# Prompt attention on one core: the selected branch's scores stand between two groups of transposes, and the compressed branch comes last in a unit

## The reference, cut to what matters

```python
def nsa_chunk(q, gate, qpos, kc, vc, cend, ks_blk, vs_blk, kw, vw, wpos, overlap, rel_bias):
    ...
    s_c = jnp.einsum('bcgqd,bngd->bcgqn', q, kc).astype(jnp.float32) * scale
    ...
    p_c = masked_softmax(s_c, (dist_c >= 0)[None, :, None, None, :])
    o_c = jnp.einsum('bcgqn,bngd->bcgqd', p_c.astype(vc.dtype), vc)
    ...
    s_s = jnp.einsum('bcgqd,bcgkd->bcgqk', q, k_sel).astype(jnp.float32) * scale
    ...
    o_s = jnp.einsum('bcgqk,bcgkd->bcgqd', p_s.astype(v_sel.dtype), v_sel)
    ...
    o_w = jnp.einsum('bcgqw,bwgd->bcgqd', p_w.astype(vw.dtype), vw)
    g = jax.nn.sigmoid(gate.astype(jnp.float32))
    o = g[..., 0:1] * o_c + g[..., 1:2] * o_s + g[..., 2:3] * o_w
    return o.astype(q.dtype)
```

## Time and profile before

| | us |
|---|---|
| median of 3 runs | 1875.83 (1871.49 to 1879.88) |
| the profiled execution, its time | 1881.08 |
| the profiled execution, its span on the core | 1879.3 |
| PE busy / PEld busy / DVE busy / ACT busy | 1772.3 / 1685.5 / 816.1 / 525.9 |
| prompt attention, from the first maximum to the last final | 211.5 to 332.6 |

### The profile page before, as it was taken

One profiled execution on the slowest core, in us unless ns is written; L12 is line 12 of the kernel. 1 busy time (PEld: TensorE's weight loads), 2 busy tenths in 40 slices (PEclk: granted clock), 3 DMA queues, 4 the chain that ended last, 5 costly groups with the idle time before them and its releaser, 6 DMA issues. The chain is left out here.

```text
span 1879.3 us, 35977 instructions
## 1 busy us (share of the span) xinstructions
PE 1772.3 (94%) x15724; PEld 1685.5 (90%) x15724; DVE 816.1 (43%) x1650; ACT 525.9 (28%) x896; POOL 702.7 (37%) x282
## 2 busy tenths in 40 slices
PE   6989788789978998999999999999999999999997
PEld 6987677559856997899999999999999999999997
DVE  4162487223483444465530355443246455024421
ACT  5132365223331222322221222322223222112211
POOL 1200000013213111465553465656565565445541
PEclk8987699889979998899999999999999999999999
DMA  5640330423201000222223222332222222232222
GB/s 146 111 70 23 128 100 24 124 76 92 74 9 47 4 4 27 68 68 90 84 68 96 90 69 64 95 104 75 90 86 72 88 70 74 85 100 81 74 71 77
DMA packets 158252, 140.84 MB, mean 75 GB/s; under 512 B 16170, under 2 KB 153806, under 8 KB 157710
## 3 DMA queue, kind: packets, MB, share of 16 engines
q1 hardware_dynamic: 158094, 138.53, 25.2%
HBM read 132.62 MB, written 10.02 MB: 76 GB/s over the span
## 5 line engine op out<-in xcount | busy, mean ns | idle before, releaser
L271 POOL TENSOR_TENSOR w_lo<-w_raw,w_hi 128x2048 fp32r<-128x2048 f32 (+3 forms) x109 | 458.8, 4209 | 798.8 <-ACT w_hi L265 798.6
L310 PE MATMUL ps<-h_hi,w_hi 128*128 128x288 f32 x1792 | 385.1, 296 | 0.0
L310 PE MATMUL ps<-h_lo,w_hi 128*128 128x288 f32 x1792 | 384.6, 295 | 0.0
L310 PE MATMUL ps<-h_hi,w_lo 128*128 128x288 f32 x1792 | 384.4, 295 | 0.0
L265 ACT ACTIVATE w_hi<-w_raw 128x2048 fp32r<-128x2048 f32 (+3 forms) x109 | 190.0, 1743 | 510.1 <-PE ps L310 460.0
L310 PEld LDWEIGHTS ps<-h_hi,w_hi 128*128 128x128 f32 x1792 | 287.2, 188 | 0.3
L310 PEld LDWEIGHTS ps<-h_lo,w_hi 128*128 128x128 f32 x1792 | 287.2, 188 | 0.0
L310 PEld LDWEIGHTS ps<-h_hi,w_lo 128*128 128x128 f32 x1792 | 287.0, 188 | 0.0
L419 DVE TENSOR_TENSOR xT<-ps,xT 128x576 f32<-128x576 f32 x48 | 35.7, 757 | 265.9 <-PE ps L310 265.9
L310 PE MATMUL ps<-g_hi,w_hi 128*128 128x288 f32 x704 | 151.1, 295 | 0.0
L310 PE MATMUL ps<-g_lo,w_hi 128*128 128x288 f32 x704 | 151.0, 295 | 0.0
(11 more groups left out here) (500 smaller groups left out, 3016.3 us busy)
## 6 DMA issues: line engine op xcount, KB each, us to landing
w_raw<-in_ffn_up SPq DMA_DIRECT2D x44, 1024.0 KB, 5.1
w_raw<-in_ffn_down SPq DMA_DIRECT2D x16, 768.0 KB, 4.8
w_raw<-in_w_in_odd SPq DMA_DIRECT2D x12, 1024.0 KB, 5.1
w_raw<-in_ffn_down SPq DMA_DIRECT2D x16, 640.0 KB, 4.4
w_raw<-in_w_in_even SPq DMA_DIRECT2D x7, 1024.0 KB, 5.4
w_raw<-in_w_in_even SPq DMA_DIRECT2D x6, 872.0 KB, 9.9
BT<-rv SPq DMA_DIRECT2D x8, 520.0 KB, 3.5
seg<-in_cache_cmp_kv SPq DMA_DIRECT2D x32, 128.0 KB
```

What stands on the lines that cost most here:

```text
L271: pool.tensor_tensor(slab_view(wlo[slot], st), slab_view(raw[slot], st), slab_view(whi[slot], st).bitcast(F32), ALU.subtract).then_inc(w_l ...
L310: last = pe.matmul(ps[:, bank + 2 * j + half, 0:HT], w[slot][:, c:c + 128], x[:, xs + t, half * HT:(half + 1) * HT], start=(t == 0 and n = ...
```

## The change

PE's queue in unit u gets another order. The selected transposes come first and signal a semaphore of their own, `pts_ready`. Then come the selected scores of unit u + 2, then the window's transposes and the compressed one (`pt_ready`), then the other scores of u + 2. The outputs are in the order selected, window, compressed, and each waits for its own copy only. ACT copies `PTs` first, on `pts_ready`, and `PTc` second, on `pt_ready`. The selected scores wait for the maximum of unit u instead of u + 1 (their bank alternates with s). DVE's queue keeps its order; its copy `PTw` still waits for `pt_ready`. No matmul, copy or transfer is added or removed.

```diff
-                    def scores(u):
+                    def scores(u, branches):
                         h, qt, s = u // 4, u % 4, u % 2
                         g, hh = h // 4, h % 4
-                        if u >= 1:
-                            pe.wait_ge(s_taken, u)
+                        if u >= 2:
+                            pe.wait_ge(s_taken, u - 1)
...
                         for n, (out, keys) in enumerate(jobs):
+                            if (n == 0) != (branches == "selected"):
+                                continue
+                            if n == 2 and u >= 1:
+                                pe.wait_ge(s_taken, u)
                             if n == 2 and u >= 2:
                                 pe.wait_ge(ptc_act, u - 1)
...
+                        for kt in range(qt + 1):
+                            last = pe.transpose(ps[:, 5, 128 * kt:128 * kt + 128], sS[s][:, 128 * kt:128 * kt + 128], ident[:, :])
+                        last.then_inc(pts_ready, 1)
+                        if u + 2 < U:
+                            scores(u + 2, "selected")
+                        if u >= 1:
                             pe.wait_ge(pt_dve, u)
                         for kt in range(qt + 1):
-                            pe.transpose(ps[:, 5, 128 * kt:128 * kt + 128], sS[s][:, 128 * kt:128 * kt + 128], ident[:, :])
                             pe.transpose(ps[:, 6, 128 * kt:128 * kt + 128], sW[s][:, 128 * kt:128 * kt + 128], ident[:, :])
                         if u + 2 <= U:
                             pe.wait_ge(s_taken, u + 2)
+                        if u >= 1:
+                            pe.wait_ge(ptc_act, u)
                         pe.transpose(ps[0:32, 4, 256:384], sC[s][:, :], ident[:, :]).then_inc(pt_ready, 1)
                         if u + 2 < U:
-                            scores(u + 2)
+                            scores(u + 2, "others")
                         pe.wait_ge(pt_act, u + 1)
-                        pe.wait_ge(pt_dve, u + 1)
                         if u >= 1:
                             pe.wait_ge(o_taken, u)
                         O = ps[:, 7, 0:192]
-                        pe.matmul(O[:, 0:64], PTc[:, :], vc[0:32, 2, 64 * g:64 * g + 64], start=True, stop=True)
                         for n, (PT, c0) in enumerate(((PTs, 896), (PTw, 1152))):
+                            if n == 1:
+                                pe.wait_ge(pt_dve, u + 1)
                             for kt in range(qt + 1):
...
-                        last.then_inc(o_ready, 1)
+                        pe.wait_ge(ptc_act, u + 1)
+                        pe.matmul(O[:, 0:64], PTc[:, :], vc[0:32, 2, 64 * g:64 * g + 64], start=True, stop=True).then_inc(o_ready, 1)
...
-                        act.wait_ge(pt_ready, u + 1)
+                        act.wait_ge(pts_ready, u + 1)
                         if u >= 1:
                             act.wait_ge(o_ready, u)
+                        act.copy(PTs[:, 0:qt + 1, :], ps[:, 5, 0:128 * (qt + 1)].rearrange("p (a b) -> p a b", b=128)).then_inc(pt_act, 1)
+                        act.wait_ge(pt_ready, u + 1)
                         act.copy(PTc[:, :], ps[0:32, 4, 256:384]).then_inc(ptc_act, 1)
-                        act.copy(PTs[:, 0:qt + 1, :], ps[:, 5, 0:128 * (qt + 1)].rearrange("p (a b) -> p a b", b=128)).then_inc(pt_act, 1)
```

More of the change, by code:

```diff
@@ L1531, in load_group @@
                     sp.dma_start(K[1][s2][:, :, :], a["cache_win_kv"][b, 0].rearrange("(t p) k g d -> p t (k g d)", p=128)).then_inc(kvw_in[grp][s2], 16)
-            on_t, on_ev, ptc_act = sem("on_t"), sem("on_ev"), sem("ptc_act")
+            on_t, on_ev, ptc_act, pts_ready = sem("on_t"), sem("on_ev"), sem("ptc_act"), sem("pts_ready")
             U = 4 * NH
@@ L1574, in scores @@
                             last = pe.matmul(out, q, keys[1], start=False, stop=True)
-                        last.then_inc(s_ready, 1)
-                    scores(0)
-                    scores(1)
+                        if branches != "selected":
+                            last.then_inc(s_ready, 1)
+                    for u in range(2):
+                        scores(u, "selected")
+                        scores(u, "others")
                     for u in range(U):
@@ L1597, in _ @@
                         O = ps[:, 7, 0:192]
-                        pe.matmul(O[:, 0:64], PTc[:, :], vc[0:32, 2, 64 * g:64 * g + 64], start=True, stop=True)
                         for n, (PT, c0) in enumerate(((PTs, 896), (PTw, 1152))):
+                            if n == 1:
+                                pe.wait_ge(pt_dve, u + 1)
                             for kt in range(qt + 1):
-                                last = pe.matmul(O[:, 64 * (n + 1):64 * (n + 2)], PT[:, kt, :], zq[:, kt, c0 + 64 * g:c0 + 64 * g + 64],
+                                pe.matmul(O[:, 64 * (n + 1):64 * (n + 2)], PT[:, kt, :], zq[:, kt, c0 + 64 * g:c0 + 64 * g + 64],
                                                  start=(kt == 0), stop=(kt == qt))
-                        last.then_inc(o_ready, 1)
+                        pe.wait_ge(ptc_act, u + 1)
+                        pe.matmul(O[:, 0:64], PTc[:, :], vc[0:32, 2, 64 * g:64 * g + 64], start=True, stop=True).then_inc(o_ready, 1)
                     for qt in range(4):
```

## The result

The changed kernel takes 1861.5 us (median of 8 runs, 1857.5 to 1867.4), the kernel before in the same job 1875.6 us (8 runs, 1869.7 to 1882.9): ratio 0.9928, 95% interval 0.9905 to 0.9952. Measured once more later, beside other runs of before, the ratio on record was 0.9935 (0.9908 to 0.9963), though the medians of these runs (1866.3 and 1875.0) give 0.9954. The sign was right, and so was the mechanism inside a head; the size was not.

The account below looks back on a forecast made before the run. It took a ring of waits through PE, DVE and ACT as the bound in full-clock heads. 7 x (0.73 - 0.10) = 4.4 us plus 0.2 gave 4.6: 1875.83 - 4.6 = 1871.2 us, range 1864 to 1879.

Parts of the forecast that it names:

- The ring: Full-clock heads of prompt attention: a loop of waits through PE, DVE and ACT sets the pace, 13.84 us a head.
- the 13.1 to 13.3 named as the sign: Changed profile: a full-clock head should take 13.1 to 13.3 us instead of 13.84.
- The term of a full-clock head: Heads 1 to 7: each gains 0.73 us less 0.10 for late waits, 4.4 us in all.
- The charge of 0.10 for late waits: Each full-clock head: one late wait in qt = 1 or 3 costs 0.1 us; bounds nothing and 3 x 0.12.
- the first after a stop costs 0.12 more: PE's outputs: the first matmul after a stop takes 0.12 us extra, read from the compressed pair's row.
- The extra of the last head: The two last units, with no scores to issue and the longest waits, may give another 0.2 us.
- Gains nothing and loses nothing: qt = 3, selected transposes and scores first: 0.31 us earlier start pays for the scores; PTw at 272.71, was 272.74.
- the one on the clock: Short PE stops, up to 1.2 us, leave the clock at 1.00; a fall undoing the gain got little weight.
- The better clock that was allowed for: First head runs at the higher level: 11.3 us faster in all, 1864.5 us; chance 0.08.
- The other rivals: Lost cover, gain under 3 us (chance 0.20); slower by late waits, 1877 (0.05); worse clock, 1878 (0.05).

Follow-up runs that it names:

- e2: Changed kernel with the selected scores put back behind the compressed transpose; mean 1862.5 us, ratio 0.9922.
- e1: Kernel before with only the new outputs' order, a wait for each copy, and ACT's PTs copy ahead of PTc; mean 1863.8 us, ratio 0.9932.
- e8: Changed kernel with the old order of transposes and outputs in the last two of 32 units alone; mean 1870.0 us, ratio 0.9972.
- e16: Single further profile of the changed kernel with the old order in its last two units; 1872.7 us.
- e3: Kernel before plus unused filler transposes ahead of the outputs in the last two units and ahead of the closing matmuls; mean 1869.4 us, ratio 0.9957.
- e6: Changed kernel plus unused filler transposes in the last two units and ahead of the closing matmuls; mean 1862.1 us, ratio 0.9927.
- e9: Kernel before with the new transposes and outputs in the last two of 32 units alone; mean 1876.0 us, ratio 1.0004.
- e11: Kernel before with the new transposes and outputs in the last eight units (heads 6 and 7) alone; mean 1872.1 us, ratio 0.9978.
- e4: Changed kernel with the selected scores again waiting for the maximum of the unit just before; mean 1865.0 us, ratio 0.9941.
- e5: Changed kernel with two of DVE's three small operations on den moved to POOL; mean 1861.2 us, ratio 0.9923.
- e15: Single further profile of the kernel before, unchanged; 1867.2 us.
- e12: Kernel before plus 14 unused filler transposes ahead of the closing matmuls only; mean 1872.6 us, ratio 0.9980.

## Why the prediction was too small

**The ring was the right one.** That finals of qt = 3, DVE's queue, ACT's exponentials and the end of qt = 3 make the head, and that the outputs' order opens it, holds. The finals of qt = 2 and 3 wait 0.22 us and not at all (forecast 0.2 and under); PE waits for `o_taken` and `p_ready`; `PTs` is copied before the compressed transpose; DVE waits 0.46 us for `pt_ready` in qt = 3 (forecast 0.5); the first head stays at its lower clock (0.56). A later head is at 13.00, just under the 13.1 to 13.3 named as the sign.

**The term of a full-clock head was mis-sized**, 0.85 us where 0.73 - 0.10 was put. The charge of 0.10 for late waits is not there: DVE waits for PE ahead of its window copy six times in nearly seven heads, in qt = 3, and in qt = 1 the copy starts right behind DVE's finals. The other 0.1 lies in the outputs of qt = 3: from their start to the finals it is 267.23 - 264.94 = 2.29 us, where 275.19 - 272.80 = 2.39 was put. In this, "the first after a stop costs 0.12 more" was read from the wrong thing. The eight selected outputs take 265.77 - 264.94 = 0.83 us now that they come first (1.06 was put) and the window's 0.99 (0.90), while the compressed pair still takes 267.12 - 266.76 = 0.36 up to PE's next row where it comes last. Most of that time belongs to the pair, not to the stop, and the errors cancel in part. The extra of the last head, 1.09 - 0.85 = 0.24, was put right at 0.2, and the first head gave 0.36 where 0 was taken and 0.7 allowed. So the block gives 0.36 + 6 x 0.85 + 1.09 = 6.55 us in the profiles and 7.9 by the product, not 4.6.

**"Gains nothing and loses nothing", said of selected transposes and scores first**, is half right: e2 shows it for the scores, but against e1 the transposes and the early copy are worth 0.43 us a head. I had put that gain under the outputs' order, where `PTs` "was copied long before".

**The step that failed is the one on the clock.** "In this trace such stops, up to 1.2 us long, left the clock at 1.00, so I give that little": the window behind this ended at 330 us, and the fall began at 331.2. The earlier trace rows showed an 8 in that slice, and the prediction says nothing of it. So the sum put the clock at the end of the block at nothing, where the runs show 4 to 6 us. The better clock that was allowed for, with a chance of 0.08, was that of the first head, which didn't change; it came at the other end, where the change shortens PE's two stops of 1.16 and 1.09 us. The Trainium skill, TensorE: Matmul & The Clock Gate, section "A second HAM failure mode: psum-queue depth-cycling", tells of a kernel in which PE idles briefly between groups of matmuls, often enough that its clock swings between the two levels. The profiles of before agree with it in part: four of them pass all the short stops of the full-clock heads at 1.00 and fall only behind the two longer ones, the fifth falls in head 6 too. The prediction weighed the rule against one profile, cut off at 330 us, and set it aside.

**What is shown of it, and what is not.** Shown: the old order in the last two units alone lowers the clock and costs 8 us (e8, e16); filling PE's stops there gives 6.5 us without any other change (e3) and nothing where the new order is in place (e6). So the clock in the last heads and the closing is a cause of the gain beside the order. Not settled is what decides a fall. The new order in the last two or eight units is not enough to keep the clock (e9, e11). Kernels with the new order of outputs in all units (after, e1, e2, e4, e5, e6) are at the lower level for 130 to 145 us in their runs, before, e8, e9 and e11 for 148 to 155. That the heads ahead count too would fit this and e15's fall in head 6; but e3 keeps its clock with the old order in all heads, and e4's profile falls with the new one. No run isolates it, and in single profiles chance isn't excluded. The falls that the profiles of before show cost about 2.7 us four times (2.54 in the closing, some 0.1 in the last head, which takes 14.16 us in e3 and e12) and 6.2 once, 3.4 us in the mean; the runs ask for 4 to 6, with an uncertainty of about 1.5 on that. Whether a remainder sits elsewhere stays open.

The other rivals fell: no cover was lost, since the heads gain more than the 0.73 us that the forecast had without any charge.

## What to carry to other kernels

Where several results wait for copies by several engines, order the consumers by when their copies are done, and give each its own wait; that was worth 0.42 us a head by itself here, and an early signal to the copying engine as much again (heads of one profile each; the times of the runs do not tell the second part from noise). Then look at TensorE's stops at the end of a stage, where the next work isn't there yet to fill them: read the granted clock past the end of the stage, in more than one profile, before saying that short stops are harmless. To split a small gain into order and clock, use the runs (their times and mean clocks), not one pair of traces.

## What was not expected of the hardware

Stops of some 1.1 us at the end of the block went with a fall to 1.2 GHz in all five profiles of before. One of them also fell in mid-block, behind heads with the usual stops, 0.74 us and less, which the same code had passed at 2.4 GHz in the other four. The size of the last stops alone doesn't tell: with 0.73, 0.67 and 1.09 us e1 stayed at 2.4 GHz, with 0.60, 0.38 and 1.09 e4 fell for 3.4 us. The time at the lower clock differs by some 10 us (standard deviation) between runs of the same kernel, and moves their times by 0.42 us for each us of it (correlation 0.87); most of the spread of this kernel's times comes from there. POOL's maximum and product on 128 x 3 numbers took 0.22 and 0.19 us in e5, little more than DVE's 0.16.
